# A fused residual, feed forward and residual block, two-tile half-column norms, and an output projection split among the last attention heads

## What is computed

```python
# end of the first block: residual of the cross attention, then a gated feed forward layer
h = h + xo @ xa_w_o
fn = rms_norm(h, norm_ffn)
g = fn @ ffn_w_gate                                # 1024 x 2816
g_conv = ffn_conv_b + sum(cw[i] * g_pad[:, i:i + s] for i in range(3))
h = h + (silu(g_conv) * (fn @ ffn_w_up)) @ ffn_w_down
# even layer: hn = rmsnorm(x, norm_w); proj = hn @ w_in (49 tiles of 128 columns); ... ; x + concat(y_a, y_b) @ w_out
# odd layer
hn = rmsnorm(x, norm_w)
q, k, v, gate = split(hn @ w_in, 4)                # 8 heads, each with two score maps
w = softmax(q1 k1) - lam * softmax(q2 k2)          # block causal, 128 queries at a time
o = rmsnorm(w @ v, subln_w) * (1 - lam_init) * silu(gate)
x = x + o @ w_out
```

## Time and profile before

| | |
|---|---|
| median of 3 runs | 3430.79 us (3429.12 to 3433.35) |
| profiled execution, its own time | 3430.47 us |
| span of the profiled execution, first to last instruction | 3428.7 us |
| PE busy | 3122.5 us (91%) |
| DVE busy | 1774.7 us (52%) |
| ACT busy | 992.6 us (29%) |
| POOL busy | 806.5 us (24%) |
| mean granted clock of PE | 0.957 |

### The profile page before, as it was taken

One profiled execution on the slowest core, in us unless ns is written; L12 is line 12 of the kernel. 1 busy time (PEld: TensorE's weight loads), 2 busy tenths in 40 slices (PEclk: granted clock), 3 DMA queues, 4 the chain that ended last, 5 costly groups with the idle time before them and its releaser, 6 DMA issues. The chain is left out here.

```text
span 3428.7 us, 38871 instructions
## 1 busy us (share of the span) xinstructions
PE 3122.5 (91%) x15406; PEld 2455.8 (72%) x15406; DVE 1774.7 (52%) x2683; ACT 992.6 (29%) x1866; POOL 806.5 (24%) x478
## 2 busy tenths in 40 slices
PE   5999898878899999999899999998998999999769
PEld 3777777666587787787677777776676777777657
DVE  4233566543632133133558887888443267777751
ACT  2332344314222011011223233424222244444430
POOL 1221000250322323323222232323132221111002
PEclk9998999999899999999899999999998999999879
DMA  2112000010111111111211111121331100000012
GB/s 105 38 35 92 13 1 13 25 62 18 51 49 43 48 44 43 49 49 50 85 50 43 68 44 68 44 74 53 141 101 62 43 31 26 32 26 26 7 62 74
DMA packets 46715, 170.28 MB, mean 50 GB/s; under 512 B 5200, under 2 KB 5472, under 8 KB 45664
## 3 DMA queue, kind: packets, MB, share of 16 engines
q1 hardware_dynamic: 44832, 161.85, 13.9%
q0 software_dynamic: 1728, 6.29, 0.5%
HBM read 145.06 MB, written 23.07 MB: 49 GB/s over the span
## 5 line engine op out<-in xcount | busy, mean ns | idle before, releaser
L176 PE MATMUL acc<-x_hi,w_hi 128*128 128x512 f32 x2064 | 855.5, 414 | 66.8 <-DVE x_lo L267 43.4
L169 POOL CAST w_hi<-w_raw 128x1024 fp32r<-128x1024 f32 x217 | 237.9, 1096 | 2555.9 <-PE acc L178 1512.8
L177 PE MATMUL acc<-x_lo,w_hi 128*128 128x512 f32 x2064 | 829.8, 402 | 0.0
L178 PE MATMUL acc<-x_hi,w_lo 128*128 128x512 f32 x2064 | 829.0, 402 | 0.0
L171 POOL TENSOR_TENSOR w_lo<-w_raw,w_hi 128x1024 fp32r<-128x1024 f32 x217 | 543.3, 2504 | 17.4
L176 PEld LDWEIGHTS acc<-x_hi,w_hi 128*128 128x128 f32 x2064 | 396.2, 192 | 191.2 <-issue 59.6
L178 PEld LDWEIGHTS acc<-x_hi,w_lo 128*128 128x128 f32 x2064 | 396.4, 192 | 97.5
L177 PEld LDWEIGHTS acc<-x_lo,w_hi 128*128 128x128 f32 x2064 | 397.8, 193 | 89.0 <-issue 1.4
L2241 DVE SCALAR_TENSOR_TENSOR acc<-ev_upad,cols,acc 128x1024 f32<-128x1024 f32 x232 | 298.2, 1285 | 4.2
L378 DVE TENSOR_TENSOR h<-h,acc 128x1024 f32 (+1 forms) x40 | 48.8, 1221 | 317.3 <-PE acc L178 317.3
L176 PE MATMUL aux<-x_hi,w_hi 128*128 128x512 f32 x448 | 193.1, 431 | 1.6 <-POOL w_lo L171 1.6
(11 more groups left out here) (495 smaller groups left out, 4974.8 us busy)
## 6 DMA issues: line engine op xcount, KB each, us to landing
w_raw<-in_stream SPq DMA_DIRECT2D x217, 512.0 KB, 3.5
h<-in_x SPq DMA_DIRECT2D x16, 512.0 KB, 9.1
spill_h<-h SPq DMA_DIRECT2D x8, 512.0 KB, 5.2
spill<-ev_zst SPq DMA_DIRECT2D x8, 512.0 KB, 3.1
h_even<-spill_h SPq DMA_DIRECT2D x8, 512.0 KB, 7.8
ev_zr<-spill SPq DMA_DIRECT2D x8, 512.0 KB, 3.5
spill_h<-h_even SPq DMA_DIRECT2D x8, 512.0 KB, 5.3
h<-spill_h SPq DMA_DIRECT2D x8, 512.0 KB, 6.4
```

Of the source, the lines that this page charges most:

```text
L169: pool.tensor_copy(k.w_hi[slot][:], k.w_raw[slot][:]).then_inc(k.w_split, 1)
L176: pe.matmul(out, w_hi, x_hi, start=start, stop=False)
L177: pe.matmul(out, w_hi, x_lo, start=False, stop=False)
L178: return pe.matmul(out, w_lo, x_hi, start=False, stop=stop)
```

## The change

It has three parts.

1. **One feed forward block.** `block_ffn` takes the place of the seven blocks from `xa_o` to the last down projection. The norm of the layer is no longer applied before the projections: `LateNorm` splits `h` times the gain, and DVE multiplies the results with the root (`ffn_root`), once for the gate (in place of ACT's copy) and once for the product with the up projection. `late_tile` makes a tile's last contraction tile last, for both column halves. The sum of squares is made behind the first gate tile.

2. **`HalfNorm` and `first_two`**, at the start of the even and of the odd layer. The norm goes through the left 512 columns of all 8 tiles, and then through the right ones. PE uses each piece for the first two streamed tiles, so 6 matmuls follow each piece. The even layer uses the second accumulator for the second tile, the odd layer four half banks.

3. **The odd output projection.** Its stream tiles hold 4 contraction tiles of two output rows. The half over heads 0 to 3 is made in 16 pieces of 12 matmuls into `aux[:, 0:HALF]`: 3 in blocks 5 to 7 of head 6, 10 in blocks 0 to 4 of head 7, 3 in blocks 5 to 7 of head 7. DVE adds each piece to `h`, and PE waits for that before the next piece. The half over heads 4 to 7 is made at the end in 8 rows of 24 matmuls. The first two rows begin with heads 4 to 6, ahead of the turn of the last head. The splits of heads 0 to 5 move to earlier blocks (`SPLIT_AT`), and the reloads of `h` come in three groups on SP's queue.

```diff
+    elif n >= STREAM["odd_out"][0]:
+        oa = STREAM["odd_out"][0]
+        part, at = divmod(n - oa, KD // 2)
+        pair = OUT_PAIRS[at]
+        src = k.stream[oa + 2 * pair:oa + 2 * pair + 2, :, part * HALF:(part + 1) * HALF].rearrange("n p c -> p n c")
+class HalfNorm:
+    def on_tensor(self, pe):
+        pe.wait_ge(self.early.summed, KD - 1)
+        for c in (0, HALF):
+            pe.matmul(self.k.aux[:, c:c + HALF], self.k.ones, self.early.acc[:, c:c + HALF], start=True, stop=True).then_inc(self.total, 1)
+    def on_scalar(self, act):
+        load_log_exp(act)
+        self.root_of(act, 0)
+        for m in range(2 * KD):
+            j, cols = self.place(m)
+            if m == 3:
+                self.root_of(act, 1)
+            act.wait_ge(self.full, m + 1)
+            act.activation(self.x_hi[:, j, cols], self.scaled[m % 2][:, 0:HALF], ACT.Copy).then_inc(self.hi, 1)
...
+def first_two(k, pe, norm, n, outs, half):
+    for i in range(2):
+        pe.wait_ge(k.w_split, (n + i) * 2 + 2)
+    for c in range(2):
+        cols = slice(c * HALF, (c + 1) * HALF)
+        for q in range(KD):
+            norm.wait_ready(pe, c, q)
+            for i in range(2):
+                at = slice(q * P, (q + 1) * P)
+                mm = product3(pe, outs[i][c], k.w_hi[(n + i) % 2][:, at], k.w_lo[(n + i) % 2][:, at],
+                              norm.x_hi[:, q, cols], norm.x_lo[:, q, cols], q == 0, q == KD - 1)
+                if q == KD - 1:
+                    mm.then_inc(k.lin_done if c else half, 1)
...
-def block_ffn_in(k, part):
+class LateNorm:
+    def high(self, act, j):
+        act.activation(self.x_hi[:, j, :], self.k.h[:, j, :], ACT.Copy, scale=self.gain_of(j)).then_inc(self.hi, 1)
+    def low(self, dve, j):
+        dve.wait_ge(self.hi, j + 1)
+        dve.scalar_tensor_tensor(self.x_lo[:, j, :], self.k.h[:, j, :], self.gain_of(j), self.x_hi[:, j, :].bitcast(F32),
+                                 ALU.mult, ALU.subtract).then_inc(self.lo, 1)
...
+def block_ffn(k):
+            def late_tile(n, x_hi, x_lo, kt, lo, count):
+                pe.wait_ge(k.w_split, n * 2 + 2)
+                pe.wait_ge(k.acc_free[slot], n // 2)
+                for qs in (range(kt - 1), range(kt - 1, kt)):
+                    for c in (0, HALF):
+                        for q in qs:
+                            if c == 0:
+                                pe.wait_ge(lo, count + q + 1)
...
+            for p, tiles in enumerate(FFN_PARTS):
+                if p == 0:
+                    late_tile(ga[p], x_hi, x_lo, KD, late.lo, 0)
+                    late.on_tensor(pe)
+                    over_tiles(pe, ga[p] + 1, da[p], tile(x_hi, x_lo, KD))
+                else:
+                    over_tiles(pe, ga[p], da[p], tile(x_hi, x_lo, KD))
+                late_tile(da[p], g_hi, g_lo, tiles, s["lo"], first[p])
+                over_tiles(pe, da[p] + 1, da[p] + KD, tile(g_hi, g_lo, tiles))
...
+                    dve.tensor_tensor(gate[:, 2:SEQ + 2], acc[:, slot, :], root[:], ALU.mult).then_inc(k.acc_free[slot], 1)
...
+                    dve.tensor_tensor(conv[:], conv[:], acc[:, other, :], ALU.mult).then_inc(k.acc_free[other], 1)
+                    dve.wait_ge(k.acc_free[other], i + ((a + 1) // 2 + 1))
+                    dve.tensor_tensor(conv[:], conv[:], root[:], ALU.mult).then_inc(s["producted"], 1)
...
+    SPLIT_AT = {(H - 2, 0): (0,), (H - 2, 1): (1, 2), (H - 2, 2): (3,), (H - 2, 3): (4,), (H - 2, 5): (5,), (H - 1, 4): (H - 2,)}
...
+            def piece(m):
+                if m % 4 == 0:
+                    pe.wait_ge(k.w_split, (oa + m // 4) * 2 + 2)
+                if m:
+                    pe.wait_ge(s["added"], m)
+                else:
+                    pe.wait_ge(s["copied"], 8 * H)
+                    pe.wait_ge(s["od_lo"], 4)
+                output(aux[:, 0:HALF], m // 4, m % 4 // 2, m % 2, range(4)).then_inc(k.lin_done if m % 4 == 3 else s["pieces"], 1)
...
+                    if n in (0, 3):
+                        for m in pieces[n // 3:n // 3 + 1]:
+                            piece(m)
...
+            for r in range(2):
+                for c in range(2):
+                    output(rows[r][c], 4, r, c, range(3))
             turn_o(H - 1, 0)
             turn_o(H - 1, 1)
+            pe.wait_ge(s["od_lo"], 8)
```

More of the change, by code:

```diff
@@ new lines, in block_ffn @@
+def block_ffn(k):
+    wa, wb = STREAM["xa_o"]
+    ga = [STREAM[f"ffn_gu{p}"][0] for p in range(len(FFN_PARTS))]
+    da = [STREAM[f"ffn_down{p}"][0] for p in range(len(FFN_PARTS))]
+    end = STREAM[f"ffn_down{len(FFN_PARTS) - 1}"][1]
+    first = [sum(FFN_PARTS[:p]) for p in range(len(FFN_PARTS))]
+    LAST = len(FFN_PARTS) - 1
+    o_hi, o_lo = k.x_hi, k.x_lo
+    x_hi, x_lo = k.at("x3_hi", 64, [P, KD, SEQ], F32R), k.at("x3_lo", 96, [P, KD, SEQ], F32R)
+    g_hi, g_lo = k.at("g_hi", 0, [P, FFN_PARTS[0], SEQ], F32R), k.at("g_lo", 32, [P, FFN_PARTS[0], SEQ], F32R)
+    squares = EarlySquares(k, "ffn")
+    gate = k.at("ffn_gate", 128, [P, SEQ + 2])
+    conv = k.at("ffn_conv", 132.25, [P, SEQ])
+    root = k.at("ffn_root", 136.25, [P, SEQ])
+    late = LateNorm(k, "fn", COLS["norm_ffn"], x_hi, x_lo, squares, root[:], k.aux)
+    k.squares = EarlySquares(k, "even")
+    reloaded, stored, summed = k.residual_sems
+    base, k.residuals = k.residuals * KD, k.residuals + 1 + len(FFN_PARTS)
+    names = "padded conved chain silued producted hi lo".split()
+    s = {n: k.own(f"ffn_{n}") for n in names}
+    acc = k.acc
@@ L1568, in _, with tile @@
         @block.tensor
         def _(pe):
[L1570 to L1576, removed]
+            def tile(x_hi, x_lo, kt):
+                return lambda n, slot, turn: linear_tile(k, pe, n, slot, turn, x_hi, x_lo, kt)
@@ new lines, in add @@
+            def add(n, done):
+                dve.wait_ge(k.lin_done, n + 1)
+                h = k.h[:, done % KD, :]
+                dve.tensor_tensor(h, h, acc[:, n % 2, :], ALU.add).then_inc(summed, 1)
+                dve.wait_ge(summed, base + done + 1)
+                dve.sem_inc(k.acc_free[n % 2], 1)
+            for j in range(KD):
+                add(wa + j, j)
+                if j:
+                    late.low(dve, j - 1)
+                    squares.add(dve, j - 1)
+            late.low(dve, KD - 1)
@@ L1616 @@
+            k.squares.add(dve, KD - 1)
+    k.release()
 G_, V_, Z_ = "g", "v", "z"
@@ L2480, in block_diff @@
     d_hi, d_lo = k.od_hi, k.od_lo
-    norm = Norm(k, k.h_even, COLS["c_norm"], x_hi, x_lo, [sc[:, i, :] for i in range(5)], sc[:, 5, :], early=k.squares)
+    norm = HalfNorm(k, "c_norm", k.h_even, COLS["c_norm"], x_hi, x_lo, [sc[:, i, :] for i in range(2)], sc[:, 2, :], k.squares)
     acc, aux = k.acc, k.aux
```

294 lines of the change are left out of this document (206 added, 88 removed).

## The result

The changed kernel takes 3339.97 us (median of 4 runs, 3334.14 to 3343.71), against 3430.44 us for the kernel before (3429.12 to 3433.35). The ratio is 0.9734, with a 95% interval of 0.9715 to 0.9752. The forecast was 3330.0, with 3316 to 3350 as its range. The measured median lies 2 us above the 3322 to 3338 to which the prediction gave a chance of 0.72, and inside the wider range. The profiled execution took 3334.14 us, which is 96.3 less than the profiled one before, where the sum had 100.4.

A forecast was written before the change was run, and what follows sets the result against it. PE, busy 91% of the span, was taken as the bound, with gains only where it stands still or runs at its lower clock. Terms -49.9 + 0.6 - 20.4 - 31.3 + 0.6 = -100.4 take 3430.47 to 3330 us; range 3316 to 3350.

The forecast's parts named there:

- The term of 1.0 us for `xa_o`: In `xa_o`, DVE's passes and POOL's split exceed the 5.6 us tile, so DVE falls behind; 1.0 us charged, ends 0 and 2.7.
- the term for the norm: Even and odd layer starts: 34.6 us each instead of 44.8, including a 3.1 us POOL wait and 1.7 for the clock.
- the upper end of the prediction: Even and odd layer norms: without the clock drop, a gain of 12 us each.
- two passes of 1.22 us: Head 6, blocks 1 and 2: earlier splits put two more passes into DVE, charged +1.5 us.
- term of 3.5 us for the gate and the split: Output projection's end: PE waits some 3.5 us for gate, `od_hi` and `od_lo` before the eighth head's part.
- two rivals that did not come true: Half norms giving nothing, and PE and DVE taking turns in the last heads: 3350 us each, chance 0.08 each.
- Half norms that give nothing: Even and odd layer starts: clock stays low through the pieces, a start takes 44 us again; 3350 us, chance 0.08.
- PE and DVE in turns: Last heads: pieces wait for DVE's additions and maxima behind them, head 7 takes 20 us more; 3350 us, chance 0.08.
- A boundary wait: Ahead of the down projections: low parts come too late, 3 times 4.5 us return; 3344 us, chance 0.05.
- A clock that gives way under dense work: PE's 784 us of dense feed forward work: at 20% low clock, +57 us, 3487 us; chance 0.01.
- The better case: Pieces cost only idle time and no clock drops behind the added waits: 5.6 + 5 us less, 3319 us; chance 0.05.

The follow-up runs named there:

- lag4: Changed kernel, but in each half norm's right half the second tile stays four contraction tiles behind the first: 3327.71 us, ratio 0.9699.
- u3_out_block: Changed kernel with the old odd output projection as a block behind the last head: 3367.68 us.
- lag_tail_late: Changed kernel with the second-tile lag, the third row's heads 4 to 6 ahead of the last wait, and later splits in head 6: 3325.08 us.
- again: The changed kernel run once more, unaltered: 3338.44 us, ratio 0.9716.
- u2_whole_norms: Changed kernel with the old whole-tile norm and one first tile in the even and odd layers: 3354.95 us.
- fill_copy: Changed kernel, but in blocks 0 to 4 of the last head the second piece stands between turn and weighing: 3339.57 us, ratio 0.9725.
- tail_fill: Changed kernel, but PE makes heads 4 to 6 of the third output row ahead of the last low part's wait: 3334.84 us, ratio 0.972.
- again2: The changed kernel unaltered, run again for comparison on the same chip as later kernels: 3335.04 us.
- wait_first: Changed kernel, but each part's first down tile waits for all its low parts before its first matmul: 3364.47 us, ratio 0.9797.
- pool_low: Changed kernel, but POOL instead of DVE makes the low parts of heads 0 to 4: 3352.0 us, ratio 0.9765.

## Why the prediction was right

- **What bounds the kernel: right.** Where PE's idle stretches and the low clock went, the time went. DVE's 104 us more cost some 2 us in head 6, where it sets the pace, and 0.6 in `xa_o`.
- **Part 1, forecast -49.9 and a stage of 788.7: measured -50.2 and 788.38.** The late tiles hid the chain in full, and without them PE waited 7.50 us. In the pairs the pass with the root took 3.27 us on the mean beside POOL, where the sum had 1.22, and it cost nothing: DVE is busy for 353 of the stage's 788 us. The term of 1.0 us for `xa_o` was in truth 0.6, and for another reason. The prediction put the whole of POOL's split, 3.4 us, in the way of DVE's passes. But the CAST, 1.05 us of it, falls on the addition, which takes 1.21 us all the same, and only the subtraction of 2.4 us holds DVE up. The low part takes 3.19 us, a tile's three passes just fill the 5.6 us of the tile, and DVE does not fall further behind. The timeline of DVE in the changed kernel, in two tiles of `xa_o`, then the first wait of PE:

```profile
884.58 1.21 DVE L1752 TENSOR_TENSOR h<-h,acc 128x1024 f32<-128x1024 f32 x1
885.94 3.19 DVE L1639 SCALAR_TENSOR_TENSOR x_lo<-h,cols,x_hi 128x1024 fp32r<-128x1024 f32 x1
889.05 1.21 DVE L226 TENSOR_TENSOR ffn_sum<-ffn_sum,ffn_sq 128x1024 f32<-128x1024 f32 x1
890.18 1.21 DVE L1752 TENSOR_TENSOR h<-h,acc 128x1024 f32<-128x1024 f32 x1
...
894.78 0.50 PE L185 MATMUL acc<-x_hi,w_hi 128*128 128x512 f32 x1 [0.60 <-DVE x_lo L1639]
```

- **Part 2, forecast -10.1 and -10.3: measured -9.6 and -9.0** (the windows are 11.8 and 12.1 shorter, and 2.25 and 3.04 are given back behind them). The window of 32.9 us is what the sum had (29.8 + 3.1), with 2.95 for the wait where 3.1 was charged. The clock behind the wait was charged 1.7 and took 1.7 in the third tile of both layers. So the term for the norm was right, 34.6 forecast and 34.5 measured. The other 0.6 and 1.4 us given back lie further back in the layers, in code that did not change, where the clock moves from one execution to the next by as much, and no run shows that the change caused them. Without the wait and its drop the two layers save 13.4 and 12.1 us (`lag4`), where the upper end of the prediction was 12 each.
- **Part 3, forecast -31.3, or -30.7 with the end of the program: the windows give -28.0.** Undoing it costs 31.1, but 3.0 of that is the spread of heads 6 and 7 in `u3_out_block`. Three terms were too small. Head 7 became 17.9 us longer, not 16.6. There a piece of 12 matmuls takes 2.88 to 2.98 us and not 2.8, mainly since its second matmul starts 0.32 us behind the first and not 0.23; that is 1.4 us over 13 pieces. PE's other work is 0.7 more than the 24.3 us that were read off head 5, and the idle time is 4.7 us and not 5.6. Blocks 0 to 4 of head 6 became 2.4 us longer, not 1.5. The term charged two passes of 1.22 us at 1.5 without a reason, and on a DVE that sets the pace they are paid nearly in full: with the old splits `u3_out_block` takes 41.75 us for these blocks, 2.1 less than the changed kernel, and with one pass fewer `lag_tail_late` takes 1.0 less. The end of the program became 1.2 longer, not 0.6. The tail was forecast at 51.2 and took 51.0. Its term of 3.5 us for the gate and the split does not follow from its parts, which add up to 3.8 without any wait. PE waited 3.54, because the first of the two gate passes starts while PE still turns the other half. That it fitted is luck.
- **The sum** is 4.1 us too low against the profiled execution: 2.0 behind the norms, 1.3 in head 7, 0.9 in head 6, 0.6 at the end, 0.3 in the wait ahead of the odd layer's sum (5.24 us, 4.92 before), less what the rest gives. The other 5.8 us lie between that execution (the fastest of the four) and the median of 3339.97. They are most likely the spread of the first attention, since the profiled executions of the result and of `again` differ there alone. A forecast made against one profiled execution carries that spread, and this one took it as nothing. That the median fell into the range is so in part luck: what took the range up to 3350 was two rivals that did not come true.
- **The rivals.** Half norms that give nothing: excluded by `u2_whole_norms` (+19.9). Its price was also wrong: with 16 pieces of 2.56 us the sum's own terms give a start of some 50 us, not 44, and so 3360, outside the range. PE and DVE in turns: head 7 has at most 0.7 us idle in a place, though `fill_copy` shows that the turn-taking begins as soon as two pieces stand closer. A boundary wait: none. A clock that gives way under dense work, and a slower kernel by it: none, with 788 us at 1.00. The better case had two conditions. That no clock drops behind the added waits can be had (`lag4`, `tail_fill`). That the pieces cost only idle time was not reached.

## What to carry to other kernels

Where the densest engine waits at a boundary for a chain, keep back the last contraction step of the next tile rather than speeding up the chain: here 8 to 10 us of independent work hid a chain that PE waits 7.5 us for without it. After such a change look for the waits that are left in PE's list, since a wait costs more than its length. The matmuls behind it lost 1.7 us more to the clock after the waits of 2.95 us, 1.7 or 2.9 after that of 3.54 us, and 2.0 to 2.4 after those of 7.5 us. A different order of the same matmuls (a lag between two tiles, a row begun early) took 10 us more out. Before moving work to an idle engine, ask whether the two hinder each other: POOL was idle in head 6, and giving it DVE's passes made head 6 longer.

## What was not expected of the hardware

- The same program differed by 11 us between two executions through the clock alone (0.92 against 0.99 in 180 us), in a stage with many short gaps. Why the low stretches are longer in one run stays open.
- Behind nearly the same gap the lower clock lasts for one of two lengths. In the even layer PE waits 5.7 to 6.2 us for a transfer (`x_lo` from `spill_ya`) in every kernel. In the 15 us behind that wait the changed kernel makes 48 matmuls at a mean clock of 0.88, and `again2`, which is the same program, 36 at 0.65. That is 2.8 us. `wait_first`, `pool_low`, `u2_whole_norms` and the kernel before fall on the slow side, the others on the fast one, and `pool_low` has its edit behind this place. So an even layer of 919.9 us in the changed kernel up to its last matmul, 921.5 in `again2`, 922.5 in `wait_first` and 923.1 in `pool_low` says nothing of an edit. What decides between the two lengths stays open.
- An 8-column pass of DVE took 2.25 us instead of 0.17 beside a POOL subtraction, so what such a pass loses does not depend on its size.
